# Attention by head pairs on the two row halves of TensorE, with compact staging and one instruction for bias and maximum

## The reference

```
def attend_blocked(q, k, v, sink=None):
...
        s = jnp.einsum('bqkgd,bskd->bkgqs', qblk, k, preferred_element_type=jnp.float32) * scale
        p = softmax_logits(s, sink_b).astype(v.dtype)
        return jnp.einsum('bkgqs,bskd->bqkgd', p, v)

def softmax_logits(s, sink):
...
    m = jnp.maximum(jnp.max(s, axis=-1, keepdims=True), sink)
    e = jnp.exp(s - m)
    return e / (jnp.sum(e, axis=-1, keepdims=True) + jnp.exp(sink - m))
```

## Time and profile before

| | us |
|---|---|
| runs | 2023.18, 2024.87, 2030.37 (median 2024.87) |
| profiled execution | 2024.24, with a span of 2022.4 |
| PE busy | 1769.7 (88%) |
| DVE busy | 1233.4 (61%) |
| ACT busy | 735.6 (36%) |
| POOL busy | 289.9 (14%) |
| mean granted clock of PE | 0.924 |

### The profile page before, as it was taken

How to read it: one execution, slowest core, us unless ns; L and a number is a source line. 1 busy time by engine, 2 the same in 40 slices (tenths; PEclk the granted TensorE clock), 3 DMA queues, 4 the chain that set the end, 5 groups by cost and what they waited for, 6 DMA issues and landing times.

```text
span 2022.4 us, 34073 instructions
## 1 busy us (share of the span) xinstructions
PE 1769.7 (88%) x11558; PEld 1677.9 (83%) x11558; DVE 1233.4 (61%) x2253; ACT 735.6 (36%) x1206; POOL 289.9 (14%) x255
## 2 busy tenths in 40 slices
PE   5797799884999999999499879889949999999993
PEld 1695688873999999999399878888939999999993
DVE  4576666576777767777662166786266662366524
ACT  4530455324444224431241134444246552244310
POOL 1542321005000000000340032350050000000002
PEclk8897899996999999999899856899979999999997
DMA  8240000240333543345132110010201222122211
GB/s 309 73 158 32 6 0 0 84 165 2 105 113 126 176 139 120 108 150 181 49 105 73 42 35 0 1 40 1 73 10 63 73 83 84 63 73 73 92 43 52
DMA packets 41782, 160.49 MB, mean 79 GB/s; under 512 B 4976, under 2 KB 6000, under 8 KB 41200
## 3 DMA queue, kind: packets, MB, share of 16 engines
q1 hardware_dynamic: 38880, 152.00, 22.3%
q0 software_dynamic: 1616, 6.68, 1.0%
q10 hardware_dynamic: 1216, 0.92, 0.1%
HBM read 156.04 MB, written 3.54 MB: 79 GB/s over the span
## 4 chain that ended last, share of the span: by engine, by line
PE 42%; DVE 5%; issue 2%; ACT 1%; POOL 1%; DVEq 0%; ACTq 0%; POOLq 0%
PE ps L1371 14%; PE ps L1372 14%; PE ps L1528 3%; PE ps L1552 3%; PE ps L1410 2%; DVE x L859 1%; PE ps L1540 1%; PE ps L1468 1%; PE ps L1469 1%; DVE work L838 1%; PE ps L1423 1%; PE ps L1397 1%; PE ps L1424 1%; DVE stat L1016 1%; PE ps L1384 0%
## 5 line engine op out<-in xcount | busy, mean ns | idle before, releaser
L484 ACT ACTIVATE whi<-raw 128x1024 fp32r<-128x1024 f32 (+1 forms) x166 | 185.6, 1120 | 601.2 <-PE ps L1372 515.9
L1371 PE MATMUL ps<-hh,whi 128*128 128x320 f32 x920 | 288.1, 313 | 8.6 <-DVE wlo L771 8.6
L1371 PE MATMUL ps<-hh,wlo 128*128 128x320 f32 x920 | 284.7, 309 | 0.0
L1371 PE MATMUL ps<-hl,whi 128*128 128x320 f32 x920 | 284.7, 309 | 0.0
L1372 PE MATMUL ps<-hh,whi 128*128 128x320 f32 x920 | 284.7, 309 | 0.0
L1372 PE MATMUL ps<-hh,wlo 128*128 128x320 f32 x920 | 284.6, 309 | 0.0
L1372 PE MATMUL ps<-hl,whi 128*128 128x320 f32 x920 | 284.6, 309 | 0.0
L771 DVE TENSOR_TENSOR wlo<-raw,whi 128x1024 fp32r<-128x1024 f32 (+1 forms) x166 | 218.8, 1320 | 72.6 <-ACT whi L484 72.2
L1219 POOL TENSOR_TENSOR work<-y,work 128x640 f32<-128x640 f32 x32 | 59.7, 1870 | 1228.7 <-DVE work L838 1218.1
L1371 PEld LDWEIGHTS ps<-hh,whi 128*128 128x128 f32 x920 | 173.0, 188 | 10.6 <-DVE wlo L771 9.6
L1372 PEld LDWEIGHTS ps<-hh,whi 128*128 128x128 f32 x920 | 173.0, 188 | 1.0
(11 more groups left out here) (216 smaller groups left out, 3898.3 us busy)
## 6 DMA issues: line engine op xcount, KB each, us to landing
raw<-in_w SPq DMA_DIRECT2D x134, 512.0 KB, 3.4
work<-in_wmodt SPq DMA_DIRECT2D x54, 512.0 KB, 3.6
raw<-in_w SPq DMA_DIRECT2D x32, 704.0 KB, 4.1
ring<-in_wmodt SPq DMA_DIRECT2D x26, 512.0 KB, 3.6
work<-in_wmod SPq DMA_DIRECT2D x16, 512.0 KB, 4.5
work<-in_rpb POOLq DMA_DIRECT2D x8, 480.0 KB, 4.7
x<-in_x SPq DMA_DIRECT2D x1, 2560.0 KB, 17.9
out_x<-x SPq DMA_DIRECT2D x1, 2560.0 KB, 7.5
```

The lines of the kernel that those rows point to most:

```text
L484: nc.scalar.activation(whi[:, s, 0:kk * P], raw[:, s, 0:kk * P], ACT.Copy).then_inc(s_hi, 1)
L1371: T.matmul(bankA[s], slot(w, s, k), h[:, k, 0:HT], start=st, stop=sp_)
```

## The change

1. **Pairs of jobs, one list.** The loops and their registers are gone. `attention_units()` makes a list of units, a unit being the two heads a and b of a pair with the same t; each engine walks the list, fully written out.
2. **Scores on row halves.** `qh` and `ql` hold a chunk as it is ([P, 2, NT]), with no zeros and no memsets; POOL casts and subtracts two pieces of 128 rows a pair instead of four of 64 rows. A product reads `q[job.rows]` and `k[job.rows]`, 64 rows: rows 0 to 63 for a and 64 to 127 for b. Products alternate a, b. Head a's scores stand in PSUM banks 0 and 1, b's in 2 and 3, one set for each half.
3. **The scale and the signs.** -1/8 goes into the q gain (`gqk`) for B and into the copies of q for C and D (`unit_pair`, `copy_b`, `qk_pair`), the sink and the masks change sign, the bias is subtracted from the mask. Maxima become minima and the exponential's factor -1, so the minimum of the negated scores is the negative maximum, with no negation behind it.
4. **One instruction for mask or bias and minimum.** `tensor_tensor_reduce` adds and reduces in one: one for C (with the sink as its start value), for D one on 512 columns and one on 128, whose start value is the first's result (`s_mx`).
5. **Slots and order of staging.** `kh` and `kl` have a third slot, which C uses. POOL's order is C's first two pairs, the four masks, C's next two, D's first two (waiting for scores of C's pairs), then the bias loads, staging and masks of D's last two.

The core of the diff:

```diff
-        qh = over("qh", [P, 2, 2, NT], F32R)
-        ql = over("ql", [P, 2, 2, NT], F32R)
-        kh = over("kh", [P, 2, 6 * P], F32R)
+        qh = over("qh", [P, 2, NT], F32R)
+        ql = over("ql", [P, 2, NT], F32R)
+        kh = over("kh", [P, 3, 6 * P], F32R)
...
+            def neg_max(job):
...
+                if not job.scaled:
+                    V.tensor_reduce(negm, scores_of(job, job.lo, NT), AX.X, ALU.min).then_inc(s_neg, 1)
+                    return
...
+                    V.tensor_tensor_reduce(out=sbuf[:, job.lo:NT], in0=scores_of(job, job.lo, NT),
+                                           in1=maskc[:, m0:m0 + NT - job.lo], scale=1.0, scalar=sink[:, head:head + 1],
+                                           op0=ALU.add, op1=ALU.min, accum_out=negm).then_inc(s_neg, 1)
...
-                for q in (qh, ql):
-                    V.memset(q[DH:P, :, 0, :].bitcast(F32), 0.0).then_inc(s_qzero, 1)
-                    V.memset(q[0:DH, :, 1, :].bitcast(F32), 0.0).then_inc(s_qzero, 1)
...
+                for f, src, w in pieces:
+                    G.tensor_copy(qh[:, i, f:f + w], qk[:, qc, src:src + w]).then_inc(s_stage, 1)
...
+            def scores(unit):
...
+                if a.index > 60:
+                    pe.wait_ge(s_neg, a.index)
+                elif 0 < a.index < 60:
+                    pe.wait_ge(s_p, a.index)
...
+                for n, (q, k) in enumerate(((qh, kh), (qh, kl), (ql, kh))):
+                    for i, (c, k0, w) in enumerate(runs):
+                        for job in unit:
+                            ins = T.matmul(scores_of(job, c, c + w), q[job.rows, job.pair, job.q0:job.q0 + P],
+                                           k[job.rows, job.kslot, k0:k0 + w], start=n == 0, stop=n == 2)
...
+            def attention(layer, v):
+                units = UNITS_OF[layer]
+                scores(units[0])
+                for i, (a, b) in enumerate(units):
+                    after = units[i + 1] if i + 1 < len(units) else None
+                    if after and a.scaled:
+                        scores(after)
+                    turn_probs(a)
+                    if after and not a.scaled:
+                        scores(after)
+                    turn_probs(b)
+                    sum_values(a, v)
+                    sum_values(b, v)
```

More of the change, by code:

```diff
@@ L614, in _ @@
             value_pair(5, v0, 0)
[L616 to L647, removed]
@@ new lines, in copy_turned, with attention @@
+            def copy_turned(job):
+                j = job.index
+                if not job.prompt:
+                    act.wait_ge(s_pt, j + 1)
+                    if j >= 2:
+                        act.wait_ge(s_o, j - 1)
+                    nc.scalar.activation(pts[:, job.half, job.lo:NS], ps[:, 4, job.lo:NS],
+                                         ACT.Copy).then_inc(s_pta, 1)
+            def attention(layer):
+                for unit in UNITS_OF[layer]:
+                    for job in unit:
+                        exponent(job)
+                    for job in unit:
+                        copy_turned(job)
@@ L734, in _ @@
             p1 = UNITS[(1, "in")][0] // 2
[L735 to L736 removed]
+            with act.Fori(0, 4) as h:
+                unit_pair(h + p1, [part(qk, 2 * h + s, 0, HT) for s in range(2)], scale=-SCALE)
+            with act.Fori(0, 2) as h:
+                unit_pair(h + (p1 + 4), [part(qk, 2 * h + (8 + s), 0, HT) for s in range(2)])
             act.wait_ge(s_unit, 2 * p1 + 12 + 3)
@@ new lines, in turn_probs @@
+            def turn_probs(job):
+                j = job.index
+                pe.wait_ge(s_p, j + 1)
+                if j:
+                    pe.wait_ge(s_ptb, j)
+                if not job.prompt:
+                    if job.latent:
+                        pe.wait_ge(s_pta, job.latent)
+                    for c in range(job.lo, NS, P):
+                        T.transpose(ps[:, 4, c:c + P], pb[j % 4][:, c:c + P], ident[:, :])
+                T.transpose(ps[:, 5, 0:P], pb[j % 4][:, NS:NT], ident[:, :]).then_inc(s_pt, 1)
@@ new lines, in sum_values @@
+            def sum_values(job, v):
+                j = job.index
+                pe.wait_ge(s_ptb, j + 1)
+                if not job.prompt:
+                    pe.wait_ge(s_pta, job.latent + 1)
+                if j >= 2:
+                    pe.wait_ge(s_oe, j - 1)
+                keys = [(job.lo + P * i, t) for i, t in enumerate(job.tiles)] + [(NS, job.vctx)]
+                for i, (c, t) in enumerate(keys):
+                    last = T.matmul(ps[:, 6 + job.half, 0:DH], pts[:, job.half, c:c + P],
+                                    v[:, t, job.v_col:job.v_col + DH], start=i == 0, stop=i == len(keys) - 1)
+                last.then_inc(s_o, 1)
```

413 lines of the change are left out of this document (190 added, 223 removed).

## The result

The changed kernel takes 2091.78 us (median of four runs, 2088.81 to 2094.74) against 2024.03 for the one before: a ratio of 1.0343, with a 95% interval of 1.0302 to 1.0385. It is 3.4% slower, where 3% faster was forecast. The profiled execution has a span of 2088.9 us (before 2022.4), with a mean granted clock of 0.879 instead of 0.924.

The account below looks back on a forecast made before the run. PE was taken to set the pace, with C's cost mostly its low clock. Starts -10, B -17, C -30, D -7 sum to -64 from 2024.24: 1960 us, chance 0.43; own range 1935 to 1985, with rivals 1932 to 2018.

Parts of the forecast that it names:

- Why should it rise?: In C: two heads' scores standing together, a transpose block behind, raise the clock; 88 us against 118.1, -30.
- D's sum: Stretch D: units of 5.4 us, no wait at start or loop break; 100 us against 107.1, -7.
- Rival 1: C stays at the lower clock: C 127 us, +9 instead of -30, the whole 1999; chance 0.23.
- Rival 3: Slower: clock stays at 0.50 in B as well, C cold, D warm; the whole 2085; chance 0.13.
- Rival 2: The two row halves do not run at once, scores 1.9 us a unit; the whole 2000; chance 0.14.
- The starts: Ahead of B and C: shorter staging, no memsets; -4 and -5.8 us, about -10 together.
- The scores and switches: Each two-head unit: scores 1.1 us instead of 1.86, plus 0.3 for going between full rows and halves.
- B's sum: Stretch B: 24 latent units at 4.7 us plus prompt units, head and tail; 134 against 151.9, -17.
- The prompt unit: In B: six units with little PE work, running at their chain's length, estimated at 2.2 us each.
- D's unit: Steady unit in D: scores, turnings, stall, sums and switches, 5.4 us against 5.08 before.
- The joined instruction: On DVE: mask, scale and maximum in one instruction; one pass (0.68 us) to two (1.36), under PE's time either way.
- The stall: In C and D: turning of b waits for ScalarE's copy for a; 0.85 us in D, 0.70 and 0.55 in C.

Follow-up runs that it names:

- experiment 8: Changed kernel with C's scores on all 128 rows, k padded with zeros so each head's scores stay apart: 2036.14 us, 1.0061.
- experiment 5: Changed kernel with both heads' score products on the same 64 rows, so they cannot run at once (b's scores become a's): 2286.78 us, 1.1284.
- experiment 3: Changed kernel with scores on all 128 rows, both heads' rows summed in each product, so the two cannot run at once: 2035.55 us, 1.0032.
- experiment 1: Changed kernel with the next unit's scores between the turnings of a and b in C and D: 2053.74 us (ten runs), 1.0098.
- experiment 4: Changed kernel with next scores between the turnings in C and D, and six idle products at each pair's head in B, C and D: 2011.64 us, 0.9906.
- experiment 9: Changed kernel with C's k zero-padded to 128 rows, idle products at pair heads in B and D, D's scores between its turnings: 1999.54 us, 0.9878.
- experiment 2: Changed kernel with six idle full-row products at the head of each pair of B from the second on: 2077.24 us, 1.0231.
- experiment 10: The kernel of experiment 9 with C's scores between the turnings as well: 2017.86 us, 0.9969.
- experiment 6: The kernel of experiment 4 with more idle products ahead of B's and C's first scores and in C's latent units: 2004.35 us, 0.9895.
- experiment 7: Kernel before the change, with four idle products in the first four jobs of each of C's two loop iterations: 2019.01 us, 0.9963.

## Why the prediction was wrong

**The step that failed** is the paragraph on C's clock, "Why should it rise?", and with it D's sum, which took the full clock for granted. In C the clock never rose: 126.4 us against 88. D, with a mean clock of 0.60, took 155.6 against 100. Of the 131 us between the forecast and the profiled time these two are 38 and 55, and B is 25.

The prediction read the rise in B as the work of scores that stand close together, and the zeros in the padded q as waste. The experiments answer that for the scores in C: put back on 128 rows they bring the clock to 0.91, with half of the rows zeros in k (experiment 8), and on 64 rows in the same time as on 128 it stays at 0.50 (experiment 5). The change made the scores shorter (1.22 us for a unit of B, and not 1.86), and what was left, 90% busy in C, stood at 0.50. That the shorter time of the scores, with both halves at work at once, is what does it in the changed kernel is argued from this; experiment 5 shows the rows, and experiment 3 time and rows together.

In D the stall's order is 26 us of the loss (experiment 1). With the thin stretches at the pairs filled as well it is back at 107.2 (experiment 4), and with C at the full clock ahead of it at 105.8 (experiment 9).

**Rival 1** (C at half clock) had the mechanism of its stage and the price: +9 forecast, +8.3 measured. **Rival 3** had the right sign for the wrong place: it put the loss in B, where the clock came back after each fall, and left D warm; D lost 48 us. Its 2085 lies near the 2091.78 by luck, since it adds 69 us in B, where 7.7 were measured, and takes 7 off D. No rival had C and D cold together. **Rival 2** is out: the halves run at once.

**The starts** were right: 3.6 and 4.9 us against 4 and 5.8.

**The scores and switches** were right as a sum: 1.1 + 0.3 forecast. Measured are 1.22 up to the next transpose, and the first score starts 0.28 us behind the last transpose, where transposes follow each other at 0.11; the 0.17 between makes 1.39. But these 0.17 are not the price of going from full rows to halves. Experiment 3, whose scores stand on full rows, has the same 0.28:

```profile
251.13 0.27 PE L1547 MATMUL ps<-ident,pb 128*128 128x128 f32 x1
251.41 0.96 PE L1531 MATMUL ps<-kh,qh 128*128 128x128 f32 x4
```

On the way back the first transpose starts 0.38 us behind the last scores (230.11 to 230.49), on full rows 0.24 (253.35 to 253.59), so some 0.14 there. The Trainium skill ("TensorEngine Tiling (Array Packing)", Tiling Modes, Key Properties) says that a change of tiling mode drains TensorE; the 0.14 agree with a short drain on the way back, and on the way in these rows show none. The same list says that different tiles load and multiply in parallel; the 1 to 9 ns between the two products of a couple agree.

**B's sum** was too low even at the full clock: experiment 2, with no fall, has 145.7 against 134. The unit is 4.98, not 4.7, some 7 us over 24 units: from the first value product to the next transpose it is 2.39 us (231.09 to 233.48) and not 2.12, and a turning is 0.60 and not 0.55. The prompt unit, put at 2.2 by an estimate, costs 3.7, 9 us over six. The head and the tail, put at 8, came out some 4 lower, by what is left of 145.7. PE's timeline in experiment 2, from the prompt unit's scores to the next unit's:

```profile
263.63 0.33 PE L1531 MATMUL ps<-kh,qh 64*128 64x128 f32 x2
...
267.36 0.61 PE L1531 MATMUL ps<-kh,qh 64*128 64x128 f32 x4
```

The falls of the clock at the pairs add the other 14. The prediction named what stands behind the scores' wait on PE, but did not follow that list to the change of pair, where nothing stands there.

**D's unit** at the full clock is 5.63 us. The prediction's terms add up to 5.47, which it wrote as 5.4, so at the full clock D would have been some 4 us over its sum of 100; most of the other 52 is the clock, whose mean was 0.60.

**The joined instruction** was one pass, the lower end. Its group on 512 columns in D, after, and the reading of its result:

```profile
L1008 DVE CUSTOM_DVE_ANT_0 pb<-ps,work 128x512 f32<-128x512 f32 x32 | 22.1, 691 | 0.3 <-issue 0.3
L1008 DVE DVE_READ_ACCUMULATOR2_ANT stat<- 128x1 f32 x32 | 2.7, 83 | 0.0
```

0.69 us with 0.08 for reading the result, against 0.68 for the masked pass alone. DVE's 29 us less in D came mostly from it, and none of them stood on the path.

**The stall** was right: 0.78 us measured, 0.85 forecast. Once C's rows were full, the order with the stall was the better one there (experiments 9 and 10).

**What stays open.** The scatter of experiment 1, 30 us in ten runs, and B's falls at four changes of pair in one run and five in another say that the moments at which the clock falls and comes back differ between runs; why, no run here shows. Nor do the runs tell the number of rows from the shape of the product, or say why C of the kernel before, on full rows, took 38.6 us to rise. It was not tried to hold the clock in C with both heads on halves by making the value sums denser.

## What to carry to other kernels

Before you take useless work off TensorE, read the granted clock by stage, and do not take it for granted in the sum that the shortened stage will have it: the busy share did not tell it here (90% at 0.50). A stage bound by small products can lose more from a clock of 0.50 than packing gains (57 us in C and D here, against 6 in B where its clock was held). Two mends helped here: products that nobody reads, put where the engine waits, and full rows kept in a stage that the packing had left at 0.50. Try both, since their gains did not come as forecast (7 us each in experiments 6 and 7, where 21 to 34 were). Where a double buffer is given up, follow the waiting engine's list to the thinnest unit, not only through the steady one.

## What the runs showed of the hardware that was not expected

- The same score products in the same time left B at 0.95 on 128 rows and at 0.50 on 64 (2035.55 and 2286.78 us for the whole).
- Rows of zeros went with the same clock as rows of numbers: C ran at 0.91 in 93.2 us with k padded with zeros and at 0.92 in 92.9 with both heads' rows, against 0.50 in 126.6 on halves.
- Full rows alone did not hold it: C of the kernel before, with q padded with zeros, stood at 0.50 through 38.6 us.
- PE can be busy 90% of 126 us and stay at 0.50 throughout.
- Products on the two row halves started within 1 to 9 ns of each other in the unit shown; the way from halves back to full rows cost some 0.14 us more than full rows to full rows, the way in nothing more.
